# A two-block transformer in two-part float32: the ring of weights moved by 32 bytes, and the order of three products changed in half of the chunks

## The chip, the cores and the metric

The kernel runs on one core of a Trainium2 chip. TensorE (PE) multiplies, VectorE (DVE), ScalarE (ACT) and GpSimd (POOL) work element by element, SyncE (SP) issues most transfers. The metric is the device time in microseconds of one execution, lower is better. One execution was also profiled; its trace gives the start and the duration of each instruction.

## The reference, cut to what matters

Two blocks of two layers each work on one sequence of 512 tokens with 1024 features, all in float32. Nearly all the arithmetic is products of activations with weights:

```python
# first block, per layer
proj = h @ w_in[l]                       # 1024 x 2594
h = layer_norm(DEEPNORM_ALPHA * h + mixed @ w_out[l], ln1_g[l], ln1_b[l])
ff = jnp.square(jax.nn.relu(h @ w_up[l])) @ w_down[l]     # 1024 x 4096, 4096 x 1024
h = layer_norm(DEEPNORM_ALPHA * h + ff, ln2_g[l], ln2_b[l])
# second block, per layer
h = h + 0.5 * rms_norm(swiglu(rms_norm(h, g[0]), ffn_wi[i, 0], ffn_wo[i, 0]), g[1])
h = h + rms_norm(mixer(rms_norm(h, g[2])), g[3])
h = h + 0.5 * rms_norm(swiglu(rms_norm(h, g[4]), ffn_wi[i, 1], ffn_wo[i, 1]), g[5])
h = h + rms_norm(e * sigmoid(rms_norm(h, g[6]) @ ple_gate[i]), g[7])      # e = p[i] @ ple_proj[i]
```

`swiglu` has two inner matrices of 1024 x 2816 and one outer of 2816 x 1024. The mixers (sparse, gated linear and pooling attention in the first block, dilated and windowed attention in the second) add smaller products between activations.

## The kernel before

Activations lie with features on the 128 partitions and the 512 tokens along the row. The weights come from memory as a stream of 538 units. A unit is 128 x 1024 float32: eight slices of 128 x 128, one for each chunk of 128 input features. Each float32 weight and activation is split in a high part of type float32r and a low part, the rest. A product with a weight slice is then three matmuls of 128 x 128 by 128 x 512 that add up in one PSUM bank: high by high, high by low, low by high. `piece` (L916) issues them, in lines L920, L921 and L922. In what follows a "product" is one such matmul.

The activations that are multiplied by weights lie in `x` (chunk `kc`, then part 0 for high and 1 for low, then 512 tokens) and in `mid`, `ao`, `bo` and `px` in the same form. `by_lines` (L910) reorders the 512 tokens of a matmul's moving operand and of its result: with four elements, 16 bytes, as a line, it takes lines 0, 4, 8 and so on first, then 1, 5, 9, and so on.

The weights pass through a ring of four places. SP loads unit n into `raw0` to `raw3` when the unit four before is used up (`unit_done`). ACT copies it into `wh`, rounded to float32r (L1652, `hi_done`), and DVE subtracts it from `raw` and writes the low part `wl` over `raw` itself (L2153, `split_done`). TensorE waits once per unit for `split_done` and then issues the 24 products of its eight slices. Twelve units, among them the second of most sections of the stream, have places of their own outside the ring, `raw_apart`, `wl_apart` and `wh_apart`.

All buffers have addresses given by hand: `at` puts a buffer at the running `place[0]`, or at `offset`. `x` starts at byte 32896 of each partition. After `x` and `y`, `place[0]` is 82048; `place[0] += 192` (L434) moves the ring to 82240 (`raw`, `wl`) and 98624 (`wh`). The difference from `x` to each of these is 192 more than a multiple of 512, and a weight slice is 512 bytes in a row. Behind `vec`, `place[0]` is filled up so that `mid` lies a multiple of 512 behind `x` again, and so do the apart places.

`unit` (L931) issues one unit and `tile` (L942) one output tile of 128 features, of one or more units. The feed-forward stages of both blocks are runs of such tiles, partly in hardware loops. At the start of a section whose input has only just been normalised, `abreast` (L956, products in L964, L965 and L971) takes two or three tiles side by side chunk by chunk, high by high and low by high first, high by low when the low part of `x` is there. In the attention stages the order is written out by plans (`plan_n`, `plan_a`, `plan_b`) that weave weight products between the attention's own.

Of the kernel before, what the change touches and what calls it, by code (L numbers as in the profile page):

```python
# [409 lines left out]
def build(nc, stream, x_t, p_t, small, vecs, tab1, tab_a, tab_b, consts, out):  # L410
    n_units = stream.shape[0]
    with ExitStack() as ctx:
        place = [16512]

        def at(name, shape, dt=F32, offset=None):

            size = int(np.prod(shape[1:])) * 4
            if offset is None:
                offset = place[0]
                place[0] += (size + 31) // 32 * 32  # L420
            return nc.alloc_sbuf_tensor_at(name, shape, dt, offset=offset)
# [9 lines left out]
        y_at = place[0]  # L431
        y = at("y", [P, DC, S])
        px = at("px", [P, 2, 2, S], F32R, offset=x_at + 6 * 2 * S * 4)
        place[0] += 192  # L434
        raw = [at(f"raw{i}", [P, UNIT]) for i in range(4)]
        wl = [at(f"wl{i}", [P, UNIT], F32R, offset=place[0] + (i - 4) * UNIT * 4) for i in range(4)]
        wh = [at(f"wh{i}", [P, UNIT], F32R) for i in range(4)]
# [153 lines left out]
        def low_of(n):  # L591

            return place_of(n, wl, wl_apart)

        def high_of(n):

            return place_of(n, wh, wh_apart)
# [310 lines left out]
        def _(pe):  # L908
            c = Count(pe)

            def by_lines(ap):


                return ap.rearrange("p (a o w) -> p o a w", o=4, w=4)

            def piece(dst, u, col, src, kc, start, stop):  # L916

                hi, lo = high_of(u)[:, col:col + P], low_of(u)[:, col:col + P]
                dst, xh, xl = by_lines(dst), by_lines(src[:, kc, 0, :]), by_lines(src[:, kc, 1, :])
                pe.matmul(dst, hi, xh, start=start, stop=False)  # L920
                pe.matmul(dst, hi, xl, start=False, stop=False)  # L921
                return pe.matmul(dst, lo, xh, start=False, stop=stop)  # L922

            def free_tile():

# [5 lines left out]
            def unit(dst, src, chunks, start, stop, ready=None):  # L931

                pe.wait_ge(split_done, c.at("unit") + 1)
                for j, kc in enumerate(chunks):
                    if ready is not None:
                        c.wait(ready)
                    mm = piece(dst, c.n.get("unit", 0), kc % 8 * P, src, kc, start and j == 0,
                               stop and j == len(chunks) - 1)
                mm.then_inc(unit_done, 1)
                c.tick("unit")  # L940
# [37 lines left out]
            def first_tiles(order, summed=True, before=None):  # L978

                u = c.n["unit"]  # L980
                width = max(t for t, _ in order)
                for t, kc in order:
                    if kc == 0:
                        if before is not None:
                            before(t)
                        free_tile()
                        pe.wait_ge(split_done, u + t + 1)
                    if t < width:
                        abreast(u, t, kc, width, summed)
                        continue  # L990
                    mm = piece(bank[c.homes[t][0]][:, :], u + t, kc * P, x, kc, kc == 0, kc == 7)
                    if kc == 7:
                        mm.then_inc(unit_done, 1)
                        c.tick("unit")
# [284 lines left out]
            def dense_n(layer, n, order):  # L1279

                m, j = order[n] if n < len(order) else divmod(n, 8)
                kc, last = j, 7
                if n >= N_PROJ * 8:
                    m, j = PART_ORDER[n - N_PROJ * 8]
                    kc, last, m = MIXED[j], N_PART - 1, m + N_PROJ
                u = unit0[0] + (m if m < N_PROJ else n // 8)
                if j == 0:
                    free_tile()
                if m < N_PROJ and j == 0 or m >= N_PROJ and n % 8 == 0:
                    pe.wait_ge(split_done, u + 1)  # L1290
                if n < len(order):
                    abreast(unit0[0], m, j, 2 if layer else 1, summed=False)
                    return
                if layer == 0 and n == len(order):
                    c.wait(consts_in, 48)
                if m == 0:
                    c.wait(x_ready)
                elif m == N_PROJ:
                    if kc >= 3:
                        c.wait(x_ready)  # L1300
                    else:
                        pe.wait_ge(ot_ready, 3 * layer + kc + 1)
                mm = piece(bank[c.homes[m][0]][:, :], u, (j if m < N_PROJ else n % 8) * P, x, kc, j == 0, j == last)
                if m < N_PROJ and j == 7 or m >= N_PROJ and n % 8 == 7:
                    mm.then_inc(unit_done, 1)
                    c.tick("unit")
                elif j == last:
                    mm.then_inc(part_done, 1)
# [1810 lines left out]
```

## Time and profile before

| | us |
|---|---|
| median of 3 runs | 3295.97 |
| lowest, highest | 3291.71, 3296.3 |
| the profiled execution | 3295.67 |
| its span, first to last instruction | 3293.5 |
| TensorE matmul busy in it | 3241.8 |
| DVE, ACT, POOL busy | 1818.4, 1240.1, 332.1 |

Times in the profile are microseconds, or nanoseconds where "mean ns" stands. PE is TensorE's matmul part and PEld its weight load, which overlaps it. A matmul's recorded duration includes its drain, which lies under the next one's stream; the rate at which products follow one another is read from the difference of two starts, or from a stretch divided by the count of matmuls in it. A releaser, "<-", is the instruction that ended an idle time.

### The profile page before, as it was taken

How to read it: one execution, taken by the hardware profiler on the slowest of the kernel's cores; microseconds unless marked ns; L12 is line 12 of the kernel's file. 1: busy time of each engine (PE TensorE's matmuls, PEld its weight loads, DVE VectorE, ACT ScalarE, POOL GpSimd, SP SyncE). 2: the span in 40 equal slices, each digit the busy share in tenths (PEclk: the TensorE clock that was granted, in tenths of full speed). 3: DMA queues.
4: the chain of work that ended last, by engine and by line, in shares of the span. 5: the costliest groups of instructions: out<-in, count | busy, mean ns of one | idle time of the engine just before them, and what ended most of it. 6: DMA issues, size and time to landing. Idle time of an engine off the chain costs nothing.

```text
span 3293.5 us, 43153 instructions
## 1 busy us (share of the span) xinstructions
PE 3241.8 (98%) x16870; PEld 2642.0 (80%) x16870; DVE 1818.4 (55%) x2946; ACT 1240.1 (38%) x1882; POOL 332.1 (10%) x242
## 2 busy tenths in 40 slices
PE   8999999999999999999999999999999999999999
PEld 7768888776788888888788778888888886788887
DVE  6776334677752446443666664435644367654436
ACT  3355232425542324332333343324433235533325
POOL 0300000231100020000223100000000012000001
PEclk9999999999999999999999999999999999999999
DMA  4112232321132232223322222332232321133332
GB/s 169 65 46 77 96 102 97 132 73 46 46 107 98 96 103 83 98 99 109 111 71 71 69 84 97 102 108 97 90 102 96 109 99 46 59 102 102 102 109 83
DMA packets 81433, 300.39 MB, mean 91 GB/s; under 512 B 9040, under 2 KB 9040, under 8 KB 80640
## 3 DMA queue, kind: packets, MB, share of 16 engines
q1 hardware_dynamic: 78624, 284.20, 25.9%
q0 software_dynamic: 1568, 11.98, 0.9%
q8 instruction: 105, 1.72, 0.2%
q10 hardware_dynamic: 1088, 2.10, 0.2%
q14 instruction: 48, 0.39, 0.0%
HBM read 296.14 MB, written 2.10 MB: 91 GB/s over the span
## 4 chain that ended last, share of the span: by engine, by line
PE 89%; DVE 5%; ACT 3%; issue 2%; POOL 1%; DMA 1%; POOLq 0%; ACTq 0%; DVEq 0%
PE bank L920 25%; PE bank L922 25%; PE bank L921 25%; PE bank L964 2%; PE bank L971 2%; PE bank L965 2%; ACT sc L1824 1%; PE bank L1248 1%; DVE wl L2153 1%; PE bank L1489 1%; PE bank L1501 1%; PE bank L1229 1%; PE bank L1544 1%; ACT wh L1652 1%; PE bank L1263 1%
## 5 line engine op out<-in xcount | busy, mean ns | idle before, releaser
L920 PE MATMUL bank<-x,wh 128*128 128x512 f32 x2616 | 1023.0, 391 | 4.7 <-DVE wl L2153 2.9
L922 PE MATMUL bank<-x,wl 128*128 128x512 f32 x2616 | 999.4, 382 | 0.0
L921 PE MATMUL bank<-x,wh 128*128 128x512 f32 x2616 | 999.0, 382 | 0.0
L2153 DVE TENSOR_TENSOR wl<-raw,wh 128x1024 fp32r<-128x1024 f32 x526 | 669.7, 1274 | 518.2 <-ACT wh L1652 516.9
L1652 ACT ACTIVATE wh<-raw 128x1024 fp32r<-128x1024 f32 x526 | 554.4, 1054 | 1065.5 <-PE bank L922 1013.8
L920 PEld LDWEIGHTS bank<-x,wh 128*128 128x128 f32 x2616 | 490.9, 188 | 111.9 <-issue 23.0
L922 PEld LDWEIGHTS bank<-x,wl 128*128 128x128 f32 x2616 | 490.6, 188 | 88.9
L921 PEld LDWEIGHTS bank<-x,wh 128*128 128x128 f32 x2616 | 491.4, 188 | 85.6 <-issue 3.8
L920 PE MATMUL bank<-mid,wh 128*128 128x512 f32 x1216 | 465.5, 383 | 1.2 <-DVE wl L2153 1.2
L922 PE MATMUL bank<-mid,wl 128*128 128x512 f32 x1216 | 463.7, 381 | 0.0
L921 PE MATMUL bank<-mid,wh 128*128 128x512 f32 x1216 | 463.7, 381 | 0.0
L920 PEld LDWEIGHTS bank<-mid,wh 128*128 128x128 f32 x1216 | 228.1, 188 | 43.7 <-DVE wl L2153 2.1
L921 PEld LDWEIGHTS bank<-mid,wh 128*128 128x128 f32 x1216 | 228.1, 188 | 41.7 <-issue 1.0
L922 PEld LDWEIGHTS bank<-mid,wl 128*128 128x128 f32 x1216 | 228.1, 188 | 40.9
L2297 DVE TENSOR_TENSOR prod<-bank,rs_in 128x512 f32<-128x512 f32 x88 | 60.8, 691 | 220.4 <-PE bank L922 220.4
L2169 DVE TENSOR_TENSOR mid<-prod,mid 128x512 f32 (+1 forms) x152 | 104.9, 690 | 89.3 <-ACT mid L1965 86.5
L711 POOL TENSOR_TENSOR acc<-sq,sq 128x512 f32<-128x512 f32 x8 | 11.1, 1389 | 1249.8 <-ACT sq L1769 1249.8
L1965 ACT ACTIVATE mid<-prod 128x512 f32 (+1 forms) x88 | 55.5, 630 | 174.9 <-DVE prod L2683 174.9
L2635 DVE TENSOR_TENSOR prod<-tmp,bank 128x512 f32<-128x512 f32 x64 | 44.0, 687 | 137.7 <-ACT tmp L1915 137.7
L1915 ACT ACTIVATE tmp<-bank 128x512 f32<-128x512 f32 x64 | 38.0, 595 | 173.3 <-PE bank L922 173.3
L964 PE MATMUL bank<-x,wh 128*128 128x512 f32 x200 | 79.3, 396 | 13.4 <-DVE wl L2153 7.0
L2297 DVE TENSOR_TENSOR tmp<-bank,rs_in 128x512 f32<-128x512 f32 x88 | 60.8, 691 | 45.9 <-PE bank L922 44.8
(377 smaller groups left out, 3314.4 us busy)
## 6 DMA issues: line engine op xcount, KB each, us to landing
raw<-stream SPq DMA_DIRECT2D x526, 512.0 KB, 3.3
raw_apart<-stream SPq DMA_DIRECT2D x12, 512.0 KB, 3.7
sm<-small POOLq DMA_DIRECT2D x2, 2144.0 KB, 10.5
tb<-tab POOLq DMA_DIRECT2D x2, 1728.0 KB, 14.8
h<-x_t ACTq DMA_DIRECT2D x4, 512.0 KB, 6.8
out_t<-h SPq DMA_DIRECT2D x8, 256.0 KB, 2.7
tba<-tab_a POOLq DMA_DIRECT2D x1, 1152.0 KB, 7.7
pf<-p_t POOLq DMA_DIRECT2D x2, 512.0 KB, 6.0
```

The source lines that it names most:

```text
L920: pe.matmul(dst, hi, xh, start=start, stop=False)
L921: pe.matmul(dst, hi, xl, start=False, stop=False)
L922: return pe.matmul(dst, lo, xh, start=False, stop=stop)
L964: pe.matmul(dst, hi, xh, start=kc == 0, stop=False)
L965: pe.matmul(dst, lo, xh, start=False, stop=False)
L971: mm = pe.matmul(dst, hi, xl, start=False, stop=kc == 7)
L1652: act.activation(high_of(n)[:, :], raw_of(n)[:, :], ACT.Copy).then_inc(hi_done, 1)
L1965: act.activation(mid[:, i * 2 + k, 0, :], prod[k][:, :], ACT.Copy).then_inc(mid_hi, 1)
L2153: dve.tensor_tensor(low_of(n)[:, :], raw_of(n)[:, :], high_of(n)[:, :].bitcast(F32), ALU.subtract).then_inc(split_done, 1)
L2169: dve.tensor_tensor(dst, src, hi.bitcast(F32), ALU.subtract).then_inc(done, 1)
L2297: free(dve.tensor_tensor(dst, bank[c.peek()][:, :], rs_in[:, :], ALU.mult))
L2635: free(dve.tensor_tensor(prod[k % 2][:, :], tmp[k % 2][:, :], b[:, :], ALU.mult))
```

## The change

The ring starts 224 bytes behind `y` and no longer 192: `raw`, `wl` and `wh`, and behind them `sq`, `tmp`, `prod`, `acc`, `rs`, `rs_in`, `ident`, `ones` and `vec`, lie 32 bytes further on. From `mid` on all is where it was, since the padding before it shrinks by 32 bytes. And in `piece` the three products of a chunk keep their order in chunks 0 to 3 of each eight; in chunks 4 to 7 low by high comes before high by low. The last product of the chunk, whichever it is, carries `stop` and the increment.

```diff
@@ -431,7 +431,7 @@
         y_at = place[0]
         y = at("y", [P, DC, S])
         px = at("px", [P, 2, 2, S], F32R, offset=x_at + 6 * 2 * S * 4)
-        place[0] += 192
+        place[0] += 224
         raw = [at(f"raw{i}", [P, UNIT]) for i in range(4)]
@@ -918,8 +918,11 @@
                 hi, lo = high_of(u)[:, col:col + P], low_of(u)[:, col:col + P]
                 dst, xh, xl = by_lines(dst), by_lines(src[:, kc, 0, :]), by_lines(src[:, kc, 1, :])
                 pe.matmul(dst, hi, xh, start=start, stop=False)
-                pe.matmul(dst, hi, xl, start=False, stop=False)
-                return pe.matmul(dst, lo, xh, start=False, stop=stop)
+                if kc % 8 < 4:
+                    pe.matmul(dst, hi, xl, start=False, stop=False)
+                    return pe.matmul(dst, lo, xh, start=False, stop=stop)
+                pe.matmul(dst, lo, xh, start=False, stop=False)
+                return pe.matmul(dst, hi, xl, start=False, stop=stop)
```

On TensorE, in the middle of a unit of a feed-forward stage of the first block, chunk 3 and chunk 4 are issued like this in the kernel before; the names are the result, the moving operand and the weights:

```order
L920 MATMUL bank<-mid,wh_61 128x4x32x4
L921 MATMUL bank<-mid,wh_61 128x4x32x4
L922 MATMUL bank<-mid,wl_57 128x4x32x4
L920 MATMUL bank<-mid,wh_61 128x4x32x4
L921 MATMUL bank<-mid,wh_61 128x4x32x4
L922 MATMUL bank<-mid,wl_57 128x4x32x4
```

And in the changed kernel, at the same place, where L922 and L923 are the old order's lines and L924 and L925 the new one's:

```order
L920 MATMUL bank<-mid,wh_61 128x4x32x4
L922 MATMUL bank<-mid,wh_61 128x4x32x4
L923 MATMUL bank<-mid,wl_57 128x4x32x4
L920 MATMUL bank<-mid,wh_61 128x4x32x4
L924 MATMUL bank<-mid,wl_57 128x4x32x4
L925 MATMUL bank<-mid,wh_61 128x4x32x4
```

In the second of the two chunks the product with the low weights `wl` has moved from third place to second; nothing else is in another place. The other engines issue the same instructions in the same order.

## Rows read from the trace of the kernel before

**Rows 1.** The page: TensorE's busy time, its granted clock, the chain that ended last.
```profile
PE 3241.8 (98%) x16870; PEld 2642.0 (80%) x16870; DVE 1818.4 (55%) x2946; ACT 1240.1 (38%) x1882; POOL 332.1 (10%) x242
...
PEclk9999999999999999999999999999999999999999
...
PE 89%; DVE 5%; ACT 3%; issue 2%; POOL 1%; DMA 1%; POOLq 0%; ACTq 0%; DVEq 0%
PE bank L920 25%; PE bank L922 25%; PE bank L921 25%; PE bank L964 2%; PE bank L971 2%; PE bank L965 2%; ACT sc L1824 1%; PE bank L1248 1%; DVE wl L2153 1%; PE bank L1489 1%; PE bank L1501 1%; PE bank L1229 1%; PE bank L1544 1%; ACT wh L1652 1%; PE bank L1263 1%
```

**Rows 2.** The page, costliest groups: line, names, count, busy us, mean ns, idle before.
```profile
L920 PE MATMUL bank<-x,wh 128*128 128x512 f32 x2616 | 1023.0, 391 | 4.7 <-DVE wl L2153 2.9
L922 PE MATMUL bank<-x,wl 128*128 128x512 f32 x2616 | 999.4, 382 | 0.0
L921 PE MATMUL bank<-x,wh 128*128 128x512 f32 x2616 | 999.0, 382 | 0.0
...
L920 PE MATMUL bank<-mid,wh 128*128 128x512 f32 x1216 | 465.5, 383 | 1.2 <-DVE wl L2153 1.2
L922 PE MATMUL bank<-mid,wl 128*128 128x512 f32 x1216 | 463.7, 381 | 0.0
L921 PE MATMUL bank<-mid,wh 128*128 128x512 f32 x1216 | 463.7, 381 | 0.0
```

**Rows 3.** Instructions in order of time around 1400 us: start, duration, instruction.
```profile
1399.67 0.38 PE L920 MATMUL bank<-x,wh 128*128 128x512 f32 x1
...
1400.33 0.38 PE L920 MATMUL bank<-x,wh 128*128 128x512 f32 x1
```

**Rows 4.** Windows: length, PE, PEld, DVE, ACT, POOL busy (instructions), clock, DMA share, GB/s.
```profile
293.40:582.20 288.80, 288.80 (x1297) 242.93 (x1298) 119.22 (x131) 90.50 (x118) 3.87 (x3) 1.00 0.30 100
910.30:1200.00 289.70, 289.69 (x1297) 243.03 (x1298) 119.21 (x131) 90.57 (x118) 3.86 (x3) 1.00 0.30 100
1270.00:1590.00 320.00, 320.00 (x1457) 273.03 (x1456) 140.15 (x156) 96.83 (x115) 7.75 (x6) 1.00 0.31 104
```

**Rows 5.** Instructions in order of time where two long stretches begin.
```profile
292.96 0.38 PE L922 MATMUL bank<-x,wl 128*128 128x512 f32 x1
293.38 0.49 PE L920 MATMUL bank<-x,wh 128*128 128x512 f32 x1
...
909.80 0.38 PE L922 MATMUL bank<-x,wl 128*128 128x512 f32 x1
910.31 0.46 PE L920 MATMUL bank<-x,wh 128*128 128x512 f32 x1
```

**Rows 6.** The same where weights from an apart place begin.
```profile
2292.89 0.38 PE L920 MATMUL bank<-x,wh 128*128 128x512 f32 x1
...
2293.33 0.39 PE L922 MATMUL bank<-x,wl 128*128 128x512 f32 x1
2293.56 0.40 PE L920 MATMUL bank<-x,wh_apart 128*128 128x512 f32 x1
2293.80 0.39 PE L921 MATMUL bank<-x,wh_apart 128*128 128x512 f32 x1
...
2295.39 0.39 PE L922 MATMUL bank<-x,wl_apart 128*128 128x512 f32 x1
```

**Rows 7.** Instructions of the tile `wl_apart`: duration minimum/median/maximum in ns.
```profile
L922 PEld LDWEIGHTS bank<-x,wl_apart x16: 187/188/188, 2293.8 to 3262.0; 128*128 128x128 f32 x16
```

**Rows 8.** Groups by line and form: the products of `abreast`.
```profile
L964 PE MATMUL bank<-x,wh 128*128 128x512 f32 x200 | 79.3, 396 | 13.4 <-DVE wl L2153 7.0 <-ACT x L1718 4.5 <-ACT x L1700 2.0
L965 PE MATMUL bank<-x,wl 128*128 128x512 f32 x200 | 77.6, 388 | 0.0
...
L971 PE MATMUL bank<-x,wh 128*128 128x512 f32 x200 | 71.7, 390 | 1.6 <-DVE x L2198 1.6
...
L964 PE MATMUL bank<-x,wh_apart 128*128 128x512 f32 x64 | 24.9, 389 | 0.0
```

**Rows 9.** Groups by line in the stretch 1270 to 1590 us.
```profile
L921 PE MATMUL bank<-x,wh 128*128 128x512 f32 x314 | 119.3, 380 | 0.0
```

## The prediction, made before the changed kernel ran

> **What bounds the kernel now.** I read the page first, then the windows of the long stretches, then single instructions. TensorE's matmuls cover 3241.8 us of the 3293.5 us span and 89% of the chain that ended last, three quarters of it in lines L920, L921 and L922, the three products of `piece` [rows 1]. These lines hardly wait: the idle time before all 2616 L920 products on `x` is 4.7 us, before those on `mid` 1.2 us, and none stands before L921 and L922 [rows 2]. The clock is the full 2.4 GHz in every slice of the span [rows 1], and the DMA engines are at three tenths in the long stretches [rows 4]. So only the time from one product's start to the next one's, its cadence, can move the total, with 11,496 products in these lines: 3 x (2616 + 1216).
>
> That cadence is not one number. At 1400 us three products, from one L920 to the next, take 0.66 us, 220 ns each [rows 3]; over 1270 to 1590 us, 1457 products (less the two that only reach in) in 320.00 us make 219.9 ns [rows 4]. In the first block's two feed-forward stages 1297 products take 288.80 us and 289.70 us, so 222.7 and 223.4 ns [rows 4]. The code is the same, `unit` called by `tile`; DVE and ACT run at the same share or less there (119 of 289 us, against 140 of 320 us), no wait stands inside, and each stretch holds its cadence from its first microsecond to its end. The stages differ in how they were entered, after a pause of some tenths of a microsecond: 0.42 us between the starts before 293.38 us, 0.51 us before 910.31 us [rows 5]. I read this as several stable ways for the weight load of the next product to lie against the stream of this one, and a pause that picks between them.
>
> A fourth cadence depends on place. The weights of a few units lie outside the ring, in `wl_apart` and `wh_apart`, whose distance to `x` is a multiple of 512 bytes, while the ring's is 192 more than such a multiple. The last products of the ring ahead of such a unit start 0.22 us apart (2292.89 to 2293.33 us are two); the unit's first product, at 2293.56 us, lasts 0.24 us, and the next seven, from 2293.80 to 2295.39 us, take 1.59 us: 227 ns [rows 6]. The weight loads stay at 187 to 188 ns there [rows 7], so what grows is the stream. The place of the weights within 512 bytes can therefore change the cadence, and this is what the edit touches.
>
> A rule of the Trainium skill speaks against that. Its page "TensorE: Matmul & The Clock Gate", section "Part 2: What happens when you issue a matmul", says that TensorE has two independent read ports and that loading the next weights does not steal read bandwidth from the running matmul. By it the move would change nothing. The trace does not bear it out here, by the jump from 0.22 to 0.24 us at the moment at which only the weights' place changed [rows 6]. That rule is the rival of no change below.
>
> **The change, part by part.** Instructions: none added, none removed on any engine; every wait and increment stays on the same position of its group. Nothing new is queued anywhere, and each transfer keeps its issue and its size.
>
> The order of the last four chunks. Then `lo` with `xh` comes before `hi` with `xl`. Both weight slices of a chunk have been ready since one wait at the unit's head, so no product can start earlier or later for want of data. The address of `hi` and `lo` within 512 bytes is the same, and so is that of `xh` and `xl`; the pattern of 0.22 us runs over all three lines and over the chunks alike. Mean durations of L921 and L922 are both 382 ns on `x` and both 381 ns on `mid` [rows 2]; their sums differ by 0.4 us on 2616, 0.2 ns each. Half of 11,496 products at 0.2 ns is 1 us either way. The bound from the other side is the one place where the low weights already come second, `abreast`: its products take 396, 388 and 390 ns [rows 8], so 8 ns over the 382 of `piece`. 5748 products at 8 ns would be +46 us. I take 0, not 8 ns, since every third slice loaded in much of that stage is an apart one (389 ns at L964 with `wh_apart` [rows 8]) and since it waits on `x`; the upper end is kept as a rival.
>
> The ring 32 bytes further on. The distance to `x` and `mid` becomes 224 beyond a multiple of 512. `mid` stays where it was, since the padding ahead of it absorbs the 32 bytes. `sq`, `tmp`, `prod`, `acc`, `rs` and the constants move along; DVE is busy 119 and ACT 91 of 288.8 us in such a stretch [rows 4], so I cost that at 0, under the cover of products that never wait for them there; without that cover it would be whatever their instructions grow by.
>
> What is at stake is the mean above 220 ns. A product in a stretch of 219.9 ns is recorded with a duration of 380 ns, since its drain lies under the next one's stream [rows 9]. On `x`, L921 and L922 average (999.0 + 999.4) / 5232 = 381.95 ns, so 1.95 ns too much; over 7848 products 15.3 us. On `mid`, 463.7 / 1216 = 381.3 ns, 1.3 ns too much; over 3648 products 4.8 us. Together 20.1 us. Were all at 220 ns, the profiled execution of 3295.67 us would take 3275.6 us. The two slow long stretches alone give 1297 x (222.7 - 220.0) = 3.5 us and 1297 x (223.4 - 220.0) = 4.4 us, together 7.9 us: 3287.8 us. No trace shows distance 224. Its price is bounded by the cadences that are there: 219.9 and 227 ns, so -20 us to (7.0 x 11,496 = 80.5, less the 20.1 now paid) +60 us. Below nothing it can also go: single steps of 0.22 us down to 0.21 us stand inside the slower cadences, so a cadence of some 218 ns is not excluded, which would be -43 us.
>
> **Rivals.**
>
> A, faster: at 224 the products fall into the 220 ns way more often, above all in the first block. For it: 220 ns is held by the same code for 1500 products at a time, so a small shift of what the pause picks is enough. Time between 3275.6 and 3287.8 us, middle 3281.7; on the median of 3295.97, 0.3 more: 3282.
>
> B, no change: 32 bytes do not change how load and stream meet (or nothing of the place matters within the ring), and the order does nothing. For it: hi and lo, x and mid, all chunks behave alike, 512 bytes apart. 3296, give or take the 4.6 us that three runs span.
>
> C, slower: at 224 the way that a pause picks is one of the longer ones also in the second block's feed-forward stages, which now run at 220. Place: the second block's four feed-forward stages, the first of which stands in [rows 4]. For it: the other distance on record, a multiple of 512, is slower at once, in spite of entering from 220 ns. Against: 224 is nearer to 192 than to it. All at 223.4: 11,496 x 3.4 = 39.1, less 20.1: +19, 3315 us. All at 227: 3356 us. It decides from a mean cadence of 221.75 ns (20.1 us / 11,496 above 220).
>
> D, slower by the order: loading low weights beside `xh` twice running costs what `abreast` shows. At half its 8 ns, +23 us: 3319 us; in full 3342 us. Against it is all that is said of the order above.
>
> **How the numbers follow.** A 0.40 (of it 0.06 below 3262), B 0.24, C 0.30 (0.10 above 3332), D 0.06 (0.02 above 3332). The forecast is A's, 3282 us. A measurement of this kernel tells about 0.2%, 6.6 us, from no change: faster 0.40, same 0.24, slower 0.36. Range 3262 to 3332, which leaves out 0.18; as the signs are split, A's own range is 3270 to 3289.
>
> **What would show it.** The windows of 293 to 582 us and 910 to 1200 us: 1297 products in 285.3 us if A holds, 289 if B, and the second block's long stages at 219.9 ns in both. C shows in those, as from 1270 us on: 1457 products in over 325 us. D shows as a mean that differs between chunks 0 to 3 and 4 to 7 of one unit, which A, B and C all exclude. Idle before L920 stays near 5 us in each case; if it grows by more than 5 us, or if ACT or DVE take longer per instruction, my cost of 0 for the moved buffers was wrong. The forecast is wrong if the new distance has a cadence of its own that no row here shows, under 219 or over 224 ns.

## The result: 24.5 us slower, and the profile after

| | before | after |
|---|---|---|
| median, us | 3295.53 | 3320.05 |
| lowest, highest (6 runs each) | 3289.25, 3297.53 | 3307.26, 3324.34 |
| the profiled execution | 3295.67 | 3324.34 |
| its span | 3293.5 | 3322.3 |

The ratio of the times is 1.0071, with an interval of 1.0055 to 1.0087: slower. The time lies inside the predicted range and on the other side of no change than the forecast. It is the case that rival C describes.

Three views of the page of the changed kernel first: the engines, the chain that ended last, and the costliest groups. They answer to [rows 1, 2]. L920, L922 and L923 are the old order, L924 and L925 the new one; L1655 and L2156 are ACT's and DVE's split of a unit.

```profile
PE 3271.0 (98%) x16870; PEld 2637.7 (79%) x16870; DVE 1819.5 (55%) x2946; ACT 1242.2 (37%) x1882; POOL 331.3 (10%) x242
...
PE 89%; DVE 5%; ACT 3%; issue 2%; POOL 1%; DMA 0%; POOLq 0%; ACTq 0%; DVEq 0%
...
L920 PE MATMUL bank<-x,wh 128*128 128x512 f32 x2616 | 1030.5, 394 | 4.0 <-DVE wl L2156 2.5
L1655 ACT ACTIVATE wh<-raw 128x1024 fp32r<-128x1024 f32 x526 | 555.6, 1057 | 1092.4 <-PE bank L925 1035.7
L2156 DVE TENSOR_TENSOR wl<-raw,wh 128x1024 fp32r<-128x1024 f32 x526 | 670.5, 1276 | 526.3 <-ACT wh L1655 525.0
...
L922 PE MATMUL bank<-x,wh 128*128 128x512 f32 x1308 | 503.7, 385 | 0.0
L923 PE MATMUL bank<-x,wl 128*128 128x512 f32 x1308 | 503.7, 385 | 0.0
L924 PE MATMUL bank<-x,wl 128*128 128x512 f32 x1308 | 503.0, 385 | 0.0
L925 PE MATMUL bank<-x,wh 128*128 128x512 f32 x1308 | 502.7, 384 | 0.0
L920 PE MATMUL bank<-mid,wh 128*128 128x512 f32 x1216 | 469.7, 386 | 0.8 <-DVE wl L2156 0.8
```

TensorE's matmuls cover 29.2 us more (3271.0 against 3241.8), and the span is 28.8 us longer: the loss is in the products. The products wait no longer than before (4.0 us ahead of L920 on `x`, 4.7 before), TensorE still holds 89% of the chain. Each product of `piece` is recorded some 3 ns longer (384 to 386 ns against 381 to 383, L920 on `x` 394 against 391). The two lines of the new order stand at 384 and 385 ns and the two of the old at 385: nothing separates the halves of a unit.

Next the windows of the three long stretches that [rows 4] shows of before; the third has the same bounds, the other two are moved to where the stage now lies. The columns are those of [rows 4].

```profile
292.70:578.10 285.40, 285.40 (x1297) 242.61 (x1298) 119.15 (x132) 90.80 (x119) 3.83 (x3) 1.00 0.30 102
905.70:1197.80 292.10, 292.09 (x1296) 242.44 (x1297) 119.16 (x131) 90.87 (x118) 3.85 (x3) 1.00 0.30 99
1270.00:1590.00 320.00, 320.00 (x1422) 265.57 (x1421) 137.12 (x151) 94.91 (x113) 7.75 (x6) 1.00 0.30 100
```

The first stretch took 288.8 us and takes 285.4 us for its 1297 products: 220 ns each, which is what the forecast hoped for. The second took 289.7 us for 1297 and now takes 292.1 us for 1296. In the third, 320 us held 1457 products and now hold 1422: 225.3 ns (320 / (1422 - 2) = 225.35) where there were 219.9. The clock is full in all of them and the DMA engines are at 0.30 of their time as before.

Single products near 1400 us, to be read beside [rows 3] (start, duration, instruction):

```profile
1399.65 0.39 PE L920 MATMUL bank<-x,wh 128*128 128x512 f32 x1
1399.88 0.39 PE L922 MATMUL bank<-x,wh 128*128 128x512 f32 x1
1400.11 0.39 PE L923 MATMUL bank<-x,wl 128*128 128x512 f32 x1
1400.34 0.38 PE L920 MATMUL bank<-x,wh 128*128 128x512 f32 x1
1400.56 0.38 PE L922 MATMUL bank<-x,wh 128*128 128x512 f32 x1
1400.78 0.39 PE L923 MATMUL bank<-x,wl 128*128 128x512 f32 x1
1401.01 0.39 PE L920 MATMUL bank<-x,wh 128*128 128x512 f32 x1
```

From L920 to L920 it is now 0.69 and 0.67 us, where it was 0.66. The trace holds the starts to the nanosecond, and there the gaps (from one product's start to the next one's) come in fixed rounds. In the slow stretches of after the round is 219, 230, 224, 232, 222 ns, mean 225.3, over and over for some 1500 gaps; in the fast one it is 221, 221, 218 ns, mean 220.0. A round of five over chunks of three products walks through every chunk, every line and both halves of a unit, so it belongs to none of them.

The six long stretches hold the whole loss. Mean gap in each, from those starts, in the one profiled execution of each kernel:

| stretch, gaps | before | after |
|---|---|---|
| first block, layer 0 feed-forward, 1294 | 222.67 | 220.0 |
| first block, layer 1 feed-forward, 1294 | 223.38 | 225.33 |
| second block, first feed-forward, 1495 | 220.0 | 225.33 |
| second, 1501 | 220.0 | 225.34 |
| third, 1495 | 220.0 | 225.34 |
| fourth, 1501 | 220.0 | 225.34 |

That is -3.5, +2.5 and 4 x 8.0 = +32.0 us, together +31.1 us with rounding; outside these stretches the two executions differ by -2.3 us, and the sum is the 28.8 us of the spans.

### The profile page after: what moved, and what is told of

It reads as the page before. It is cut to its first block, busy times and chain, and to the rows that moved or that the text cites. A ratio compares the mean times of both kernels' runs of the same rounds, so it can differ in the third digit from the quotient of the medians.

```text
span 3322.3 us, 43153 instructions
## 1 busy us (share of the span) xinstructions
PE 3271.0 (98%) x16870; PEld 2637.7 (79%) x16870; DVE 1819.5 (55%) x2946; ACT 1242.2 (37%) x1882; POOL 331.3 (10%) x242
## 4 chain that ended last, share of the span: by engine, by line
PE 89%; DVE 5%; ACT 3%; issue 2%; POOL 1%; DMA 0%; POOLq 0%; ACTq 0%; DVEq 0%
PE bank L920 26%; PE bank L922 13%; PE bank L923 13%; PE bank L924 12%; PE bank L925 12%; PE bank L967 2%; PE bank L968 2%; PE bank L974 2%; DVE wl L2156 1%; ACT sc L1827 1%; PE bank L1251 1%; ACT wh L1655 1%; PE bank L1492 1%; PE bank L1504 1%; PE bank L1232 1%
## 5 line engine op out<-in xcount | busy, mean ns | idle before, releaser
L920 PE MATMUL bank<-x,wh 128*128 128x512 f32 x2616 | 1030.5, 394 | 4.0 <-DVE wl L2156 2.5
L1655 ACT ACTIVATE wh<-raw 128x1024 fp32r<-128x1024 f32 x526 | 555.6, 1057 | 1092.4 <-PE bank L925 1035.7
L2156 DVE TENSOR_TENSOR wl<-raw,wh 128x1024 fp32r<-128x1024 f32 x526 | 670.5, 1276 | 526.3 <-ACT wh L1655 525.0
L920 PEld LDWEIGHTS bank<-x,wh 128*128 128x128 f32 x2616 | 490.0, 187 | 118.8 <-issue 22.9
L922 PE MATMUL bank<-x,wh 128*128 128x512 f32 x1308 | 503.7, 385 | 0.0
L923 PE MATMUL bank<-x,wl 128*128 128x512 f32 x1308 | 503.7, 385 | 0.0
L924 PE MATMUL bank<-x,wl 128*128 128x512 f32 x1308 | 503.0, 385 | 0.0
L925 PE MATMUL bank<-x,wh 128*128 128x512 f32 x1308 | 502.7, 384 | 0.0
L920 PE MATMUL bank<-mid,wh 128*128 128x512 f32 x1216 | 469.7, 386 | 0.8 <-DVE wl L2156 0.8
L923 PEld LDWEIGHTS bank<-x,wl 128*128 128x128 f32 x1308 | 244.9, 187 | 48.4
L925 PEld LDWEIGHTS bank<-x,wh 128*128 128x128 f32 x1308 | 244.6, 187 | 48.2
L924 PEld LDWEIGHTS bank<-x,wl 128*128 128x128 f32 x1308 | 245.0, 187 | 46.9 <-issue 2.4
L922 PEld LDWEIGHTS bank<-x,wh 128*128 128x128 f32 x1308 | 245.4, 188 | 46.0 <-issue 1.4
L920 PEld LDWEIGHTS bank<-mid,wh 128*128 128x128 f32 x1216 | 227.4, 187 | 47.9 <-DVE wl L2156 1.6
L922 PE MATMUL bank<-mid,wh 128*128 128x512 f32 x640 | 246.3, 385 | 0.0
L923 PE MATMUL bank<-mid,wl 128*128 128x512 f32 x640 | 246.1, 385 | 0.0
L924 PE MATMUL bank<-mid,wl 128*128 128x512 f32 x576 | 221.7, 385 | 0.0
L925 PE MATMUL bank<-mid,wh 128*128 128x512 f32 x576 | 221.4, 384 | 0.0
L922 PEld LDWEIGHTS bank<-mid,wh 128*128 128x128 f32 x640 | 119.7, 187 | 24.4 <-issue 1.0
L923 PEld LDWEIGHTS bank<-mid,wl 128*128 128x128 f32 x640 | 119.7, 187 | 23.9
```

What stands on the lines that cost most here:

```text
L924: pe.matmul(dst, lo, xh, start=False, stop=False)
L925: return pe.matmul(dst, hi, xl, start=False, stop=stop)
L1655: act.activation(high_of(n)[:, :], raw_of(n)[:, :], ACT.Copy).then_inc(hi_done, 1)
L2156: dve.tensor_tensor(low_of(n)[:, :], raw_of(n)[:, :], high_of(n)[:, :].bitcast(F32), ALU.subtract).then_inc(split_done, 1)
```

## The experiments

A kernel is called by the head of its label: e1 is e1_place_only, m1 is m1_distances. Each time is a median, its ratio that to the kernel before on the same chip.

All gaps and means of gaps below are worked out from the starts in the traces. "The window of the second block" is 1275 to 1590 us, in its first feed-forward stage; at 220 ns it holds 1432 products, and up to eleven more where the stage begins or ends at another time, at 225.3 ns 1398 to 1400. "The windows of the first block" are 300 to 570 us and 920 to 1190 us: 1229 products at 220 ns, 1214 at 222.7, 1210 at 223.4, 1200 at 225.3.

**The two halves of the change apart.** The first kernel has the new place and the old order, the second the old place and the new order.

```diff
# e1_place_only, against the kernel before
-        place[0] += 192
+        place[0] += 224
# e2_order_only, against the kernel before: the hunk of `piece` alone
```

> The ring 224 bytes further on, with the old order of the three products in all chunks. Theory P (the place alone did it): ratio to the kernel before 1.005 to 1.009, as the changed kernel's 1.0071, and the long stretches fall into the pattern of five gaps 219, 230, 224, 232, 222 ns (225.3 ns) or the pattern of three 221, 221, 218 ns (220.0 ns). Theory O (the order did it): ratio 1.000 with gaps of 220, 223.3 and 222.7 ns. If both share it: about 1.003.

> The ring at 192 bytes, with the low weights second in chunks 4 to 7. Theory P: ratio 0.998 to 1.002, gaps in the long stretches as in the kernel before (220.0, or 222 and 225 in turn, or five gaps of 222.7 ns in the mean), none of the 219, 230, 224, 232, 222 pattern. Theory O: ratio 1.005 to 1.009.

The place alone: 3323.57 us, ratio 1.0089 [1.0076, 1.0102]. The order alone: 3292.24 us, ratio 0.9996 [0.9987, 1.0005]. Their windows of the second block, the place's first:

```profile
1275.00:1590.00 315.00, 315.00 (x1400) 261.42 (x1399) 133.60 (x148) 92.03 (x109) 7.73 (x6) 1.00 0.30 100
```
```profile
1275.00:1590.00 315.00, 314.32 (x1439) 267.66 (x1438) 136.05 (x150) 94.25 (x112) 8.88 (x8) 1.00 0.33 106
```

The place does all of it: its six long stretches have the same means as those of the changed kernel, one for one, and the slowest of the order's 12 runs (3295.71 us) is below the fastest of the place's six (3315.02 us). With the order alone all six run at 220.0 ns, the two of the first block too, so its profiled execution is at 3287.19 us; the median over 12 runs shows that this is not worth more than can be measured. Four of the 23 runs of the kernel before on that chip lie at 3287.91 to 3288.35 us, so it may take the same ways at times. Rival D is ruled out.

**Is it the ring's own address, or its distance to `x`?** Everything moved by 32 bytes, distance 192 kept:

```diff
-        place = [16512]
+        place = [16544]
```

> All buffers 32 bytes further on, x and mid too, so that the ring's own address is that of the changed kernel while its distance from x is the 192 of before; old order. Theory D (the distance between the weights and the moving operand counts): ratio 0.998 to 1.002 and the gaps of the kernel before. Theory A (the weights' own address counts): ratio 1.005 to 1.009 and the pattern of five with 225.3 ns.

3292.9 us, ratio 1.0004 [0.9993, 1.0016]; all six long stretches at 220.0 ns. The window of the second block:

```profile
1275.00:1590.00 315.00, 315.00 (x1443) 268.35 (x1441) 136.13 (x150) 93.96 (x111) 8.87 (x8) 1.00 0.33 107
```

The weights lie here where they lie in the changed kernel (82272), and nothing is lost. So the weights' own address does not do it; what e1 changes and this run does not is the distance.

**Distance 0.** If distance matters, the value that the apart places showed must be bad for the whole ring:

```diff
-        place[0] += 192
+        place[0] += 0
```

> The ring at distance 0, old order. If distance 0 has only the pattern of seven gaps (239, 225, 226, 220, 222, 221, 234 ns, mean 226.7) that the apart weights showed, all 11,496 products of piece take 226.7 ns against 221.7 on average before: +57 us, ratio 1.017, 3353 us. If that pattern belongs to the apart places and not to the distance: ratio 1.000.

3337.14 us, ratio 1.0137 [1.012, 1.0154], so slower as expected but by less than the 1.017 that 226.7 ns everywhere would give. The windows of the first block show why:

```profile
300.00:570.00 270.00, 270.00 (x1193) 223.39 (x1192) 109.47 (x121) 83.51 (x109) 2.57 (x2) 1.00 0.30 98
920.00:1190.00 270.00, 270.00 (x1211) 226.29 (x1210) 112.44 (x125) 85.91 (x113) 2.57 (x2) 1.00 0.30 98
```

The first holds 226.67 ns (a round of seven: 239, 225, 226, 220, 222, 221, 234), the second 223.33 ns (a round of four: 218, 230, 224, 221). Of the six stretches four have the way of the first window and two that of the second. So distance 0 has two ways as well, and no row of the kernel before had shown the second.

**The cadence by itself, over all distances.** A kernel of nothing but these products, 16 copies of one unit of weights at distances 0, 32, ..., 480 from `x`, each entered eight times with 48 products; it computes no part of the reference. It was run once, as were the two like it further on. Nothing else runs beside the products but a small copy on DVE between entries.

```diff
+for i in range(48):      # per distance, eight times
+    kc, j = i // 3 % 8, i % 3
+    pe.matmul(by_lines(dst), w[d][:, kc * P:kc * P + P], by_lines(x[:, kc, j == 1, :]), ...)
```

> Only products: 16 distances between weights and moving operand (0, 32, 64, up to 480 bytes beyond a multiple of 512), each entered 8 times after a pause of its own length, 48 products a time, order hi, hi, hi on the moving parts high, low, high; nothing of the reference is computed. Theory P says that each distance has a small set of steady patterns and that the pause picks one: at 192 gaps of 220.0, 222 and 225 in turn, or five of 222.7 ns; at 224 three of 220.0 or five of 225.3 ns; at 0 seven of 226.7 ns. The rival, that the patterns come from what else runs in the kernel (ACT, DVE, DMA), says one and the same gap at all distances, 216 to 220 ns. Sums of a pattern should be multiples of 6.667 ns at every distance if a free-running clock of that period takes part, and arbitrary otherwise.

The groups of its products, per distance (`w_a` is 0, `w_f` 160, `w_g` 192, `w_h` 224, `w_m` 384, `w_p` 480), and the record of one tile's weight loads:

```profile
L68 PE MATMUL bank<-x,w_a 128*128 128x512 f32 x384 | 91.2, 396 | 36.1 <-ACT x L54 34.1 <-DVE spare L76 2.0
L68 PE MATMUL bank<-x,w_m 128*128 128x512 f32 x384 | 91.0, 394 | 2.3 <-DVE spare L76 2.3
...
L68 PE MATMUL bank<-x,w_f 128*128 128x512 f32 x384 | 89.9, 391 | 2.3 <-DVE spare L76 2.3
...
L68 PE MATMUL bank<-x,w_g 128*128 128x512 f32 x384 | 87.7, 386 | 2.3 <-DVE spare L76 2.3
...
L68 PE MATMUL bank<-x,w_h 128*128 128x512 f32 x384 | 87.4, 385 | 2.3 <-DVE spare L76 2.3
L68 PE MATMUL bank<-x,w_p 128*128 128x512 f32 x384 | 87.2, 384 | 2.3 <-DVE spare L76 2.3
```
```profile
L68 PEld LDWEIGHTS bank<-x,w_n x384: 186/187/190, 1224.7 to 1317.1; 128*128 128x128 f32 x192
```

Mean of the last 36 gaps over the eight entries, ns:

| distance | 0 | 32 | 64 | 96 | 128 | 160 | 192 | 224 |
|---|---|---|---|---|---|---|---|---|
| | 226.2 | 226.6 | 227.3 | 225.7 | 228.9 | 229.4 | 222.7 | 222.0 |
| 256 more | 225.4 | 226.7 | 226.7 | 226.0 | 231.9 | 231.7 | 222.3 | 221.3 |

Six of the eight columns repeat within 0.8 ns after 256 bytes. The other two, 128 and 160, are 3.0 and 2.3 ns slower there: two entries at 384 ran at 240.0 ns, which none at 128 did, and two at 160 ran at 220.0 and 225.0 ns, where all eight at 416 ran at 231.6 or 231.7. So the mean nearly repeats every 256 bytes, but whether the sets of ways are the same is not shown. Of these places 192 and 224 are the best two in both rows, and neither has one cadence: the eight entries at 192 gave 223.8, 220.0, 223.4, 220.0, 228.3, 222.7, 220.0 and 223.4 ns, those at 224 gave 220.0, 225.3, 220.0, 225.2, 220.0, 225.2, 220.0 and 220.0. So 224 is no worse a place than 192. It has two ways where 192 has at least four, its slow one costs 5.3 ns, and in its profiled execution the changed kernel fell into the slow one in five long stretches of six.

The weight loads are recorded at 186 to 191 ns in every row, but for the run's first 13 at distance 0 (up to 339 ns, where the first products stand 427 ns apart), while the means of the gap move from 221 to 232. The Trainium skill, page "TensorE: Matmul & The Clock Gate", section "Part 2: What happens when you issue a matmul", says that loading the next weights does not take read bandwidth from the running matmul. This run does not agree for these float32r operands: with no other engine at work beside the products, only the place of the weights differs between 87.2 and 91.0 us for the same 384 products (`w_p` and `w_m`; the 91.2 us of `w_a` hold the run's first products). That it is read bandwidth that they lose is not shown.

**The order in which tokens are read, with distance.** The same kernel with the moving operand read in a row, or every second, fourth or eighth line of 16 bytes.

```diff
+ORDERS = ((1, 1), (2, 4), (4, 4), (8, 4))
+DISTANCES = (0, 192, 224, 256) * 4
```

> The same at distances 0, 192, 224 and 256 with four reading orders of the 512 columns: in a row, every second line of 16 bytes, every fourth (the kernel's), every eighth. If load and stream meet in the memory by address, the mean gap depends on the reading order as well as on the distance: in a row more than 221 ns at some distance, and some pair below 220 ns. If it is a fixed cost per product, all 16 cases lie within 1 ns of each other.

| lines taken | 0 | 192 | 224 | 256 |
|---|---|---|---|---|
| in a row | 227.6 | 228.9 | 233.3 | 226.7 |
| every second | 232.2 | 233.3 | 233.3 | 232.2 |
| every fourth (the kernel's) | 225.8 | 222.5 | 223.3 | 226.6 |
| every eighth | 246.7 | 240.0 | 248.2 | 246.7 |

The order of the stream matters as much as the distance does, and the kernel's order is the best of the four. The pair below 220 ns that the expectation held possible did not appear. The Trainium skill, page "SBUF — State Buffer", section "Specifications (TRN2)", gives 16-byte lines that want at least two hits each for full bandwidth; every order here takes four elements of a line in a row, so by that alone all four would run alike, and at one distance they lie up to 25 ns apart (223.3 and 248.2 at 224).

**Finer steps.** The same with 16 distances from 176 to 248.

```diff
+DISTANCES = (176, 184, 188, 192, 196, 200, 204, 208, 212, 216, 220, 224, 228, 232, 240, 248)
```

> Only products, distances 176, 184, 188, 192, 196, 200, 204, 208, 212, 216, 220, 224, 228, 232, 240 and 248 bytes, 8 entries each. If the memory is read in lines of 16 bytes, distances within one line (192 to 204, 208 to 220) give the same patterns unless a slice that starts inside a line costs one read more; then 196, 200 and 204 are slower than 192. If there is a distance whose only pattern is 220.0 ns or less, a kernel with the ring there beats both: 3276 us or less.

| 176 | 184 | 188 | 192 | 196 | 200 | 204 | 208 |
|---|---|---|---|---|---|---|---|
| 224.6 | 222.6 | 225.6 | 222.5 | 225.2 | 229.4 | 228.1 | 223.3 |

| 212 | 216 | 220 | 224 | 228 | 232 | 240 | 248 |
|---|---|---|---|---|---|---|---|
| 231.1 | 228.5 | 226.5 | 222.6 | 224.7 | 221.8 | 224.5 | 227.4 |

Four bytes change the mean by up to 8 ns (208 to 212). Within 16 bytes the first place is the fastest from 192 to 204 and from 208 to 220, as the expectation had it for lines of 16 bytes, but not from 224 on, where 232 is. It held 220.0 ns in six entries of eight and 227.2 in two. No distance has a way below 220 ns, none held 220.0 ns alone, and no kernel was run with the ring at 232.

**Does the pause pick the way?** If it does, a matmul more in the pause must change the outcome although it adds work. `stay_awake(1)` issues one matmul of 128 x 128 on constants (L1016, which the rows record as two, x2) ahead of the one in `pre_sum` that stands between `abreast` and the stage; `pre_sum` is passed eight times in an execution. At distance 224:

```diff
                 c.wait(sq_used, DC)
+                stay_awake(1)
                 pe.matmul(bank[3][:, :], ones[:, :], acc[:, :], start=True, stop=True).then_inc(pre_done, 1)
```

> The ring at 224, old order, and one small matmul (128 columns, ones by the identity, its result overwritten at once) more ahead of each pre-sum, which stands at the head of the second block's four long stretches and of the first block's two as far as they have one. It costs under 0.3 us each, some 3 us in all. Theory S (the start's place in time picks one of the steady patterns): some of the four long stretches of the second block change from 225.3 to 220.0 ns, each -8 us, so between -32 and 0 us against the kernel with 224 alone, with the first block's stretches left as they were. Rival (the pattern belongs to the place and the stage, not to the start): all patterns as with 224 alone, 3 us more.

3296.01 us, ratio 1.0018 [1.0004, 1.0032]: eight matmuls more, and the excess over the kernel before on the same chip is 4.6 us where the place alone had 31.1. Its ten runs spread from 3291.86 to 3309.44 us, all below the place's fastest. The way into the second block's first stage in the changed kernel, and then here (start, duration, instruction):

```profile
1260.01 0.38 PE L974 MATMUL bank<-x,wh 128*128 128x512 f32 x1
1260.23 1.02 PE L1106 MATMUL bank<-acc,ones 128*128 128x512 f32 x2
1260.69 0.78 PE L920 MATMUL bank<-x,wh 128*128 128x512 f32 x1
1261.31 0.38 PE L924 MATMUL bank<-x,wl 128*128 128x512 f32 x1
```
```profile
1266.29 0.39 PE L971 MATMUL bank<-x,wh 128*128 128x512 f32 x1
1266.51 0.38 PE L1016 MATMUL bank<-ident,ones 128*128 128x128 f32 x2
1266.73 1.02 PE L1104 MATMUL bank<-acc,ones 128*128 128x512 f32 x2
1267.19 0.78 PE L920 MATMUL bank<-x,wh 128*128 128x512 f32 x1
1267.81 0.38 PE L921 MATMUL bank<-x,wh 128*128 128x512 f32 x1
```

The pause itself looks the same to a hundredth of a microsecond. The stage behind it does not, as its windows of both blocks show:

```profile
300.00:570.00 270.00, 270.00 (x1200) 224.08 (x1199) 108.30 (x120) 83.17 (x108) 2.55 (x2) 1.00 0.30 97
920.00:1190.00 270.00, 270.00 (x1200) 224.06 (x1199) 108.24 (x120) 82.75 (x107) 2.56 (x2) 1.00 0.30 97
1275.00:1590.00 315.00, 315.00 (x1434) 267.74 (x1433) 139.34 (x155) 95.79 (x113) 7.71 (x6) 1.00 0.32 103
```

All four stages of the second block went from 225.3 to 220.0 ns (4 x 8.0 = 32 us gained), layer 0 of the first block went the other way (6.9 us lost), and layer 1 stayed slow. These are the ways of one execution, whose 3297.82 us is near the median.

Two added matmuls at 224, and one at distance 192:

> The same with two small matmuls ahead of each pre-sum. Theory S: again a new draw, so the long stretches' patterns may differ from those with none and with one; 220.0 or 225.3 ns, nothing else. Rival: 225.3 ns in the four stretches, 6 us more than with 224 alone.

> The ring at 192 as before, with one small matmul ahead of each pre-sum. Theory S: long stretches at 220.0, 222.7, 223.3 or 228.3 ns, and no longer all of the second block's at 220.0: between 0 and +30 us. Rival: all four of the second block stay at 220.0 ns, +3 us.

Two at 224: 3323.95 us, ratio 1.0089 [1.0073, 1.0106], the changed kernel's means in all six stretches again. One at 192: 3312.85 us, ratio 1.0065 [1.0048, 1.0082]; the first block's two stages went to 220.0 ns and the four of the second from 220.0 to 223.3. Windows of the second block, two at 224 and then one at 192:

```profile
1275.00:1590.00 315.00, 315.00 (x1400) 261.41 (x1399) 133.92 (x147) 92.16 (x109) 7.73 (x6) 1.00 0.31 100
```
```profile
1275.00:1590.00 315.00, 315.00 (x1412) 264.28 (x1411) 132.65 (x144) 91.00 (x107) 7.72 (x6) 1.00 0.31 103
```

So the kernel before is exposed in the same way: one small matmul in its pause, with nothing moved, costs 21 us. Its four fast stages are a property of the entry as much as of the place.

**Aiming at the last slow stretch.** With e5's matmul kept, one more behind the wait for the second unit of the first block's feed-forward, in layer 1 alone, and then in layer 0 alone:

```diff
                 pe.wait_ge(split_done, ...)
+                for _ in range(more):
+                    pe.matmul(dst[:, 0:P], ones[:, :], ident[:, :], start=True, stop=True)
...
-                            tile(x)
+                            tile(x, more=int(layer == 1 and k == 1))     # e9: layer == 0
```

> The ring at 224, old order, one small matmul ahead of each pre-sum as in the kernel with one more, and one at the head of the second tile of the second layer's first feed-forward stage, behind the wait with which that long stretch (1297 products from 905 us) begins. None and two small matmuls gave 225.3 ns behind the pre-sum and one gave 220.0, so one shifts the start by about half of a period of 6.667 ns. Theory S: this stretch, 225.3 ns in all four profiles with 224, goes to 220.0 ns, -6.9 us against the kernel with one more: 3289 us, ratio 0.999; where the first layer's stretch falls to 220 as well, 3282 us. Rival: it stays at 225.3 ns, 3296 us.

> As the last one, but the small matmul stands in the first layer's stage (from 292 us) in place of the second's. That stretch was at 220.0 ns in three of four profiles with 224. Theory S, with half a period per small matmul: it goes to 225.3 ns, and the second layer's stays at 225.3 ns: 3297 to 3303 us, ratio 1.002 to 1.004. Rival: no difference from the kernel with one more, and 220.0 ns in most of its executions.

3292.95 us (ratio 1.0001 [0.9992, 1.001]) and 3298.98 us (1.0026 [1.0015, 1.0036]). The windows of the first block, in layer 1's kernel and then in layer 0's:

```profile
300.00:570.00 270.00, 270.00 (x1229) 229.51 (x1228) 111.52 (x122) 84.42 (x109) 3.83 (x3) 1.00 0.31 101
920.00:1190.00 270.00, 270.00 (x1200) 224.04 (x1200) 105.56 (x116) 79.87 (x102) 3.58 (x3) 1.00 0.30 97
```
```profile
300.00:570.00 270.00, 270.00 (x1200) 224.08 (x1199) 108.27 (x120) 82.55 (x107) 2.56 (x2) 1.00 0.29 97
920.00:1190.00 270.00, 270.00 (x1229) 229.51 (x1228) 111.01 (x121) 83.26 (x107) 3.83 (x3) 1.00 0.31 100
```

The first aim missed: the matmul in layer 1 left layer 1 at 225.3 ns (1200 products), as the 22 gaps ahead of it were. The second hit. In layer 0 the 22 gaps ahead of the added matmul have a mean of 220.0 ns, and behind it the stretch runs at 225.3 (1200 products). The place, with L935 the added matmul:

```profile
296.75 0.38 PE L920 MATMUL bank<-x,wh 128*128 128x512 f32 x1
296.98 0.38 PE L921 MATMUL bank<-x,wh 128*128 128x512 f32 x1
297.20 0.38 PE L922 MATMUL bank<-x,wl 128*128 128x512 f32 x1
297.42 0.38 PE L935 MATMUL bank<-ident,ones 128*128 128x128 f32 x2
297.55 0.47 PE L920 MATMUL bank<-x,wh 128*128 128x512 f32 x1
```

A rule of the kind "one more matmul turns the stretch round" does not hold, since e8 has the counterexample. Nor does the code alone decide: layer 1 in e9 has e5's code and came out at 220.0 ns (1229 products) where e5 ran at 225.3, and so did layer 0 in e8. For such a difference between two kernels another draw of the same kernel would do as well, since each profile shows one execution; e9's is the fastest of its eight runs (3290.60 us, the other seven from 3298.62), so its layer 1 may be the exception. Both kernels have the second block at 220.0 ns in their profiles. Neither beats the kernel before: e8 is level with it and e9 a little slower, at the 3297 to 3303 us that the expectation gave.

**What decides at the entry.** In the traces of after, e1, e5 and e6 I took every run of at least twelve gaps of 200 to 240 ns, called its way by the mean from the seventh gap on (within 2.6 ns of 220.0 or of 225.3; two runs fit neither), and took the start of its first product modulo 6.667 ns, the step explained below. A steady drift of 1.4 to 1.8 ns per ms is taken out; 0 is where the second product of the round 221, 221, 218 starts, and the step is cut in 16 parts:

| starts in parts | stretches that went to 220.0 ns | to 225.3 ns |
|---|---|---|
| 13 to 15, 0, 1 | 136 | 12 |
| 2 | 10 | 14 |
| 3 to 8 | 15 | 143 |
| 9 to 12 | 9 | 8 |

The phase of the first product foretells the way in most cases (279 of 306 in the first and third line). In the two last kernels, which the table leaves out, it does so too (137 of 157), and the 36 long stretches of all six traces at 224 split without exception: the 17 at 220.0 ns start in parts 15.1 to 1.5, the 19 at 225.3 ns in parts 2.6 to 9.2. That covers the stretches whose code was the same and whose way was not. It is a correlation, and part of it may be the way itself, since a stretch that is in its way from the first gap has that way's phases. No run set the phase on purpose, and e8 shows that I could not.

## Why the prediction was wrong, and where it was right

**The bound was right.** The time is that of the products' cadence: 29.2 us more of busy PE and 28.8 us more of span, at the same clock and with no new wait.

**The order at 0 was right**, and taking 0 over the 8 ns of `abreast` too: e2's ratio is 0.9996, and the four lines of the two orders stand at 384 to 385 ns. What `abreast` shows is not the order's price. (The line there with the low weights second, L965, is at 388 ns, 6 over the 382 of `piece`; the 8 ns of rival D are those of L971.)

**The moved buffers at 0 were right.** ACT's copy is at 1057 ns and DVE's subtraction at 1276 ns, 3 and 2 ns longer, both still idle ahead of most units, and e3 moves them too without loss.

**That the distance matters was right**, against rival B: e1 against e3 shows it in the kernel. In m1, where `x` lies still, the place of the weights changes the gap with nothing beside.

**That a distance can have several ways and that the entry picks between them was right** as a reading of [rows 4, 5]: m1 has 220.0 and 225.3 ns at one distance, e5 and e7 move the total by more than their runs spread with one small matmul, and in e9 one such matmul stands at the point where a stretch changes from 220.0 to 225.3 ns.

**The step that failed is the choice of A over C.** The prediction took for A that "220 ns is held by the same code for 1500 products at a time, so a small shift of what the pause picks is enough". The same row speaks for C as strongly. What the pause picks was about to be drawn anew for all six long stretches, and on the record of before four of the six already stood at the floor: they could only stay or lose, 8.0 us each at what was measured, and some 5 us each (1500 x 3.4 ns), 20 us in all, at the 223.4 ns that was already on record. The two slow ones could win 7.9 us together at most; the prediction had worked that figure out and did not set it against the other side. It also set A's stretches of the second block "at 219.9 ns in both" as if the place could not touch them, though C named them. Layer 0's stage did what A said (285.4 us for 1297 products, the forecast's 285.3), the other five did what C said, at 225.3 ns. That is also the prediction's own last sign of being wrong, a cadence of the new distance over 224 ns that no row showed. With the stakes so unequal, slower was the likelier sign even at an even draw; that is argued from the sums and not shown.

**C's price was bounded rightly and its size lay between.** Expected were +19 us at 223.4 ns everywhere and +60 us at 227 ns; the new slow way has 225.3 ns, and +24.5 us by the medians and +28.7 us by the profiled executions came of it. The decisive mean gap of 221.75 ns lies between the 221.66 ns of before and the 224.08 ns of after, each over all some 12,200 gaps from 210 to 240 ns. C's sign, 1457 products in over 325 us, came as 1422 in 320.

**My doubt about distances below 220 ns was unfounded.** The single gaps of 0.21 us belong to slower rounds (217, 221, 224, 228, 223 ns, mean 222.67). None of the distances tried has a round below 220.0.

**What stays open.** What makes the gap depend on the distance, and why it nearly repeats after 256 bytes; what decides the phase at a pause; and how many of the executions of a given kernel take which ways. The profiles show one execution each, so that the spread of 3307 to 3324 us is the ways' doing is argued from its size, two stages of 8 us, and not shown.

## What to carry to other kernels

Where products run back to back, read the gap from start to start over whole stretches before and after an edit: two or three fixed values in the same code suggest that a stage is locked into one of several rounds, and an edit that adds or removes an instruction upstream may redraw them all. Then ask which stretches can still gain and which can only lose; here a change of nothing but 32 bytes, or one small matmul, moved the total by 21 to 31 us, as much as many real improvements. And when weights and moving operand are both float32 or float32r, try the distance between them modulo 256 bytes, at 4-byte steps, with each candidate entered several times.

## What the runs showed of the hardware that I had not expected

- Each of these rounds adds up to a multiple of 6.667 ns: three gaps of the 220.0 ns way take 660 ns (99 steps), five of the 225.3 ns way 1126.7 (169), two of 223.33 446.7 (67), five of 222.67 1113.3 (167), seven of 226.67 1586.7 (238). At the granted 2.4 GHz that step is 16 cycles (6.667 x 2.4). I read this as a stream held to some grid of that step, to which it can hold in more ways than one; the sums are measured, the grid is inferred from them.
- The rounds take no notice of other work: they run for 1294 to 1501 gaps, through DVE at 42% and DMA at 30% of the time, and 220.0 and 225.3 ns come back in m1, where nothing else runs beside the products.
- Extra work can shorten a kernel by far more than it takes: one matmul of 128 x 128 at eight places took 26.5 us off (31.1 us over the kernel before without them, 4.6 with them).
- Four bytes of distance are worth up to 8 ns per product, and reading every eighth line rather than every fourth 18 to 25 ns.
